# Two transformer blocks in float32 on one core: the input projections as seven block products, with their weight sums and the parameter loads moved

## What is computed

```python
# first block
x = x + 0.5 * swiglu(rms_norm(x, ffn1_norm), ffn1_w_gate, ffn1_w_up, ffn1_w_down)
proj = rms_norm(x, mix_norm) @ w_in          # 1024 x 7880: 4808 attention columns, 3072 gates
x = x + token_mixer(...)                     # three attentions on the columns of proj
x = x + 0.5 * swiglu(rms_norm(x, ffn2_norm), ffn2_w_gate, ffn2_w_up, ffn2_w_down)
# second block
x = layer_norm(x, ln_in_g, ln_in_b)
for l in range(2):
    h = x @ w_in_2[l]                        # 1024 x 1976
    cq, ckv, kr, nq, kc, vc, ks, vs, kw, vw, gl = jnp.split(h, split_at, axis=-1)
    x = layer_norm(ALPHA * x + mix(cq, ckv, ...) @ w_out[l], ...)
    x = layer_norm(ALPHA * x + memory_cross_attn(x, memn, ...), ...)
    x = layer_norm(ALPHA * x + conv_ffn(x, ...), ...)
```

## Time and profile before

| | |
|---|---|
| median of three runs | 1939.09 us (1938.17 to 1942.79) |
| the profiled execution | 1933.61 us |
| its span, first to last instruction | 1931.8 us |
| TensorE busy | 1837.9 us, 95% |
| VectorE, ScalarE, GpSimd busy | 835.2, 320.9, 152.1 us |
| mean granted TensorE clock | 0.972 of full speed |
| moved by DMA | 265.39 MB, 137 GB/s over the span |

### The profile page before, as it was taken

The page is one execution under the profiler, slowest core; times in us unless marked ns, Lnnn a source line. Parts: engine busy times, 40 slices in busy tenths (PEclk is TensorE's granted clock), DMA queues, the critical chain, the costliest instruction groups (busy, mean ns, idle before and its releaser), DMA issues.

```text
span 1931.8 us, 18805 instructions
## 1 busy us (share of the span) xinstructions
PE 1837.9 (95%) x7094; PEld 1240.4 (64%) x7094; DVE 835.2 (43%) x1907; ACT 320.9 (17%) x790; POOL 152.1 (8%) x111
## 2 busy tenths in 40 slices
PE   7999999989899999998999989999989999999997
PEld 6886444534747885446866758884448766578863
DVE  6775400243654776402730125573305520344564
ACT  1111000140601110112611210000123501210000
POOL 1221100000000222300000000001300000000010
PEclk9999999989999999997999999999997999999999
DMA  9554444511155554535034235444533053154540
GB/s 319 183 175 145 166 146 143 179 65 66 45 194 170 160 171 152 199 90 181 2 109 167 95 109 167 138 169 153 164 95 129 1 196 131 44 196 133 173 152 22
DMA packets 162489, 265.39 MB, mean 137 GB/s; under 512 B 4009, under 2 KB 105685, under 8 KB 162271
## 3 DMA queue, kind: packets, MB, share of 16 engines
q1 hardware_dynamic: 157470, 248.18, 38.2%
q0 software_dynamic: 4768, 15.48, 2.4%
q10 hardware_dynamic: 160, 0.52, 0.1%
HBM read 262.56 MB, written 1.08 MB: 136 GB/s over the span
## 4 chain that ended last, share of the span: by engine, by line
PE 90%; ACT 4%; DVE 3%; issue 1%; DVEq 1%; DMA 1%; SPq 1%; ACTq 0%
PE psum L679 22%; PE psum L704 18%; PE psum L742 14%; PE psum L802 13%; PE psum L714 7%; PE psum L920 3%; PE psum L955 3%; PE psum L853 2%; PE psum L691 2%; PE psum L937 2%; PE psum L841 1%; ACT x_t L1191 1%; PE psum L1129 1%; ACT work L1191 1%; DMA ring<-in_ffn_w_up_dram 1%
## 5 line engine op out<-in xcount | busy, mean ns | idle before, releaser
L679 PE MATMUL psum<-x_t,ring 128*128 128x256 f32 x1664 | 364.1, 382 | 4.2 <-ACT x_t L1191 4.2
L679 PEld LDWEIGHTS psum<-x_t,ring 128*128 128x128 f32 x1664 | 318.6, 192 | 49.3 <-ACT x_t L1191 5.4
L704 PE MATMUL psum<-ring,x_t 128*128 128x512 f32 (+2 forms) x672 | 283.9, 585 | 0.0
L704 PEld LDWEIGHTS psum<-ring,x_t 128*128 128x128 f32 x672 | 129.1, 194 | 152.8 <-issue 152.8
L802 PE MATMUL psum<-ring,work 128*128 128x512 f32 x352 | 160.9, 592 | 0.0
L574 POOL TENSOR_TENSOR work<-ring,work 128x1024 f32<-128x1024 f32 (+1 forms) x42 | 102.7, 2445 | 682.7 <-DVE work L1584 682.7
L714 PE MATMUL psum<-ring,x_t 128*128 128x512 f32 x320 | 140.0, 595 | 7.4 <-ACT x_t L1191 7.4
L802 PE MATMUL psum<-work 128*128 128x512 f32 x264 | 122.5, 592 | 0.0
L802 PEld LDWEIGHTS psum<-ring,work 128*128 128x128 f32 x352 | 66.6, 190 | 81.0 <-issue 80.8
L1700 DVE CUSTOM_DVE_ANT_0 work<-psum,work 128x256 f32<-128x256 f32 (+1 forms) x96 | 31.4, 364 | 194.5 <-PE psum L920 194.5
L714 PEld LDWEIGHTS psum<-ring,x_t 128*128 128x128 f32 x320 | 60.0, 190 | 81.5 <-issue 71.8
(11 more groups left out here) (224 smaller groups left out, 1988.1 us busy)
## 6 DMA issues: line engine op xcount, KB each, us to landing
ring<-in_ffn_w_up_dram SPq DMA_DIRECT2D x66, 1024.0 KB, 7.8
ring<-in_w_in_dram SPq DMA_DIRECT2D x21, 2048.0 KB, 7.9
ring<-in_ffn_w_down_dram SPq DMA_DIRECT2D x20, 2048.0 KB, 7.9
ring<-in_ffn_w_gate_dram SPq DMA_DIRECT2D x22, 1024.0 KB, 5.5
ring<-in_xa_wkv_dram SPq DMA_DIRECT2D x8, 2048.0 KB, 9.4
ring<-in_w_out_dram SPq DMA_DIRECT2D x6, 2048.0 KB, 7.8
ring<-in_xa_wq_dram SPq DMA_DIRECT2D x4, 2048.0 KB, 7.7
ring<-in_xa_wo_dram SPq DMA_DIRECT2D x4, 2048.0 KB, 7.9
```

The lines of the kernel that those rows point to most:

```text
L679: last = mm(o[:, c * T:(c + 1) * T], ring[:, n % RING, k * 512 + c * P:k * 512 + (c + 1) * P], acts[:, k, :], start=(k == 0), stop=(k == K ...
L704: last = mm(o[:, i * 512:i * 512 + width], acts[:, k, i * P:(i + 1) * P], ring[:, n % RING, c:c + width], start=(k == 0), stop=(k == kk - 1))
```

## The change

- `project` takes the place of `rows_entry` and `rows_stationary` for nine panels of the first block and three of each layer. It has the heads and tails of `expand`, without hidden rows. `last_columns` makes the 200 and the 440 columns as before, in banks 6 and 7.
- ScalarE copies product 1 of each panel (256 columns) and VectorE writes all the other columns to `P1` or `P2` (`project` under VectorE); `two_at` writes two places with one instruction.
- The first panel's weight sums get buffers of their own (`APART`: `W_MEM`, `W_MEM + 1024`, `W_L`) and are formed before the gathering adds. The second panel's come after the sums of the rows, each other one two panels ahead. A fourth buffer holds the sum that was in place.
- The four batches of turned rows at an entry use banks 4, 5, 4, 3.
- GpSimd makes the new fourth sums, does its clears after the third panel of a layer (in the first block, after the ninth), and issues the twelve parameter loads (now `parameters(l)`) after the first block's attention for layer 0, and after the second gain loads of layer 0 for layer 1.
- A layer's norm of the latent columns on VectorE comes after all three panels. ScalarE takes its root before it copies the last columns. The first heads wait for `group_free` of the third panel only.

```diff
@@ -112,8 +112,9 @@
     if B_H1 <= b < B_N2 or B_H2 <= b < E_X:
         return 4
-    if b in (B_N1 + 3, B_N3 + 3):
-        return 3
+    for b0 in (B_N1, B_N2, B_N3) + tuple(E_X + B_LAYER * l for l in range(LAYERS)):
+        if b0 <= b < b0 + 4:
+            return (4, 5, 4, 3)[b - b0]
     if b >= E_X and (b - E_X) % B_LAYER in (E_X1 - E_X, E_X1 - E_X + 1, E_X2 - E_X, E_X2 - E_X + 1):
         return 6 + (b - E_X) % 2
...
+WINS, LWINS = 9, 3
+F_UP1, F_DN1, F_WIN = 0, UPS, UPS + DOWNS
+F_UP2 = F_WIN + WINS
+F_DN2 = F_UP2 + UPS
+F_LWIN = F_DN2 + DOWNS
+F_DN = F_LWIN + LWINS
+F_LAYER = LWINS + DOWNS
+C_UP1, C_WIN, C_UP2, C_LWIN = 0, UPS, UPS + WINS, 2 * UPS + WINS
+A_UP1, A_WIN, A_UP2, A_LWIN = 0, 2, 4, 6
 FOURTH_ON_VECTOR = (F_UP1, F_UP1 + 1, F_UP2, F_UP2 + 1)
-FORM_PANELS = list(range(P_UP1, P_UP1 + UPS + DOWNS)) + list(range(P_UP2, P_UP2 + UPS + DOWNS)) + \
-    [L_DN + N_LAYER * l + d for l in range(LAYERS) for d in range(DOWNS)]
+APART = (F_WIN, F_LWIN, F_LWIN + F_LAYER)
+FORM_PANELS = list(range(P_UP1, P_WIN + WINS)) + list(range(P_UP2, P_UP2 + UPS + DOWNS)) + \
...
+        def row_corners(j):
+            c = corners(j)
+            return {1: c[1], 2: c[2], 6: c[6], 5: c[7], 7: c[5], 3: c[4], 4: c[3]}
+        def two_at(o1, o2):
+            v = W[:, o1:o1 + 256]
+            return bass.AP(v.tensor, v.offset, [list(v.ap[0]), [o2 - o1, 2], [1, 256]])
...
+            if f in APART:
+                return [w(o, chunks // 2, pitch // 2) for o in (W_MEM, W_MEM + 1024, W_L)]
...
-            pool.wait_ge(panel_done, P_WIN)
+            pool.wait_ge(panel_done, P_WIN + WINS)
...
             pool.dma_start(w(V_ALIBI, 2048), a["c_alibi"]).then_inc(t_in, 16)
+            parameters(0)
...
-            fourth_sums(range(F_UP2, F_DN))
+            fourth_sums(range(F_UP2, F_LWIN))
             for l in range(LAYERS):
-                if l:
-                    pool.wait_ge(panel_done, N_FIRST + N_LAYER * l)
-                else:
-                    pool.wait_ge(turned, B_MEM + 4)
-                    pool.wait_ge(panel_done, N_FIRST)
+                fourth_sums(range(F_LWIN + F_LAYER * l, F_DN + F_LAYER * l))
+                pool.wait_ge(panel_done, L_WIN + N_LAYER * l + LWINS)
                 nc.gpsimd.memset(W[HD:P, V_QTN:V_QTN + 8 * T], 0.0)
...
+                    if k == 1 and l + 1 < LAYERS:
+                        parameters(l + 1)
...
+            def project(n0, count, f0, g0, c0, a0, turn_tile, l=None):
+                n0, g0 = at(n0, N_LAYER, l), at(g0, G_LAYER, l)
+                acts = stationary(XT, XS, 0)
+                def product(j, p):
+                    rhs = moving(f0 + j, n0 + j, KD, 512)[p]
+                    for i in range(KD // 2):
+                        last = mm(row_corners(j)[p], acts[p][:, i, :], rhs[:, i, :], start=(i == 0), stop=(i == KD // 2 - 1))
+                    return last
+                def head(j):
+                    arrived(n0 + j)
+                    group(g0 + j)
+                    pe.wait_ge(first_out, c0 + j)
+                    product(j, 1).then_inc(first_done, 1)
+                    product(j, 2)
+                def tail(j):
+                    pe.wait_ge(forms_ready, f0 + j + 1)
+                    if j == 0:
+                        pe.wait_ge(acts_ready, a0 + 1)
+                    product(j, 6).then_inc(part_done, 1)
+                    if j == 0:
+                        pe.wait_ge(acts_ready, a0 + 2)
+                    product(j, 7)
+                    product(j, 5).then_inc(part_done, 1)
+                    pe.wait_ge(fourth_ready, f0 + j + 1)
+                    product(j, 4)
+                    product(j, 3).then_inc(panel_done, 1)
+                turn_tile(0)
+                head(0)
+                turn_tile(1)
+                head(1)
+                tail(0)
+                tail(1)
+                for j in range(2, count):
+                    head(j)
+                    tail(j)
+                pe.wait_ge(first_out, c0 + count)
+            def last_columns(n, g, width, l=None):
+                n, g = at(n, N_LAYER, l), at(g, G_LAYER, l)
+                arrived(n)
+                pe.wait_ge(group_free, g - 1)
+                for i in range(TT):
+                    for k in range(KD):
+                        last = mm(bank(6 + i)[:, 0:width], XT[:, k, i * P:(i + 1) * P],
+                                  ring[:, n % RING, k * 512:k * 512 + width], start=(k == 0), stop=(k == KD - 1))
...
-            rows_entry(P_WIN, G_WIN, 512, lambda i: turn_tile(B_N2, 3, 3, i))
-            for j in range(1, 9):
-                rows_stationary(P_WIN + j, [G_WIN + j], XT, KD, 512, 512)
-            rows_stationary(P_WIN + 9, [G_WIN + 9], XT, KD, 512, 200)
+            project(P_WIN, WINS, F_WIN, G_WIN, C_WIN, A_WIN, lambda i: turn_tile(B_N2, 3, 3, i))
+            last_columns(P_WIN + 9, G_WIN + 9, 200)
...
-                rows_entry(L_WIN, H_WIN, 512, turn_tile_of(E_X, X, 13, 9, l), l)
-                for j in range(1, 4):
-                    rows_stationary(L_WIN + j, [H_WIN + j], XT, KD, 512, min(512, N_LIN - 512 * j), l)
+                project(L_WIN, LWINS, F_LWIN + F_LAYER * l, H_WIN, C_LWIN + LWINS * l, A_LWIN + 2 * l, turn_tile_of(E_X, X, 13, 9, l), l)
+                last_columns(L_WIN + 3, H_WIN + 3, N_LIN - 1536, l)
                 pe.wait_ge(p_in, at(PARAMS, PARAMS, l))
                 for j in range(2):
                     batch(E_CW + j, [CW[0:88, j, :]], l)
-                pe.wait_ge(group_free, at(H_WIN + 4, G_LAYER, l))
+                pe.wait_ge(group_free, at(H_WIN + 3, G_LAYER, l))
                 for j in range(4):
                     batch(E_NSA + j, [P2[:, i, D_NQ + (2 * j + s) * HD:D_NQ + (2 * j + s + 1) * HD] for s in range(2) for i in range(TT)], l)
                 for j, c in enumerate((D_KC, D_VC, D_KS, D_KW)):
+                    if j == 2:
+                        pe.wait_ge(group_free, at(H_WIN + 4, G_LAYER, l))
                     batch(E_NSA + 4 + j, [P2[:, i, c + s * HD:c + (s + 1) * HD] for s in range(2) for i in range(TT)], l)
                 pe.wait_ge(rows_ready, at(16, PER_Y, l))
...
+            def project_copies(k, b0, count, c0, l_norm=None, l=None):
+                def first(j):
+                    act.wait_ge(first_done, c0 + j + 1)
+                    copy(W[:, TEMPS + 1024 * (j % 2):TEMPS + 1024 * (j % 2) + 256], corners(j)[1]).then_inc(first_out, 1)
+                rstd(k, 1, l_norm)
+                turned_rows(b0, XT, l, range(2))
+                rstd(k + 1, 1, l_norm)
+                first(0)
+                turned_rows(b0, XT, l, range(2, 4))
+                for j in range(1, count):
+                    first(j)
...
-                s1, s2, s4 = sums
+                s1, s2, s4 = sums[0:3]
+                s3 = sums[3] if len(sums) == 4 else even[:, :, a2]
                 v.tensor_tensor(s1, even[:, :, a2], odd[:, :, a2], ALU.add)
                 dr()
                 mid = v.tensor_tensor(s2, s1, even[:, :, a1], ALU.subtract)
                 dr()
-                v.tensor_tensor(even[:, :, a2], even[:, :, a1], even[:, :, a2], ALU.subtract)
+                v.tensor_tensor(s3, even[:, :, a1], even[:, :, a2], ALU.subtract)
                 return mid, v.tensor_tensor(s4, odd[:, :, a1], s2, ALU.subtract)
...
+            def project(f0, count, g0, c0, columns, row, b_last_turn):
                 dve.wait_ge(turned_out, b_last_turn)
                 mid, last = act_sums(XT, XS, 0)
+                mid.then_inc(acts_ready, 1)
+                last.then_inc(acts_ready, 1)
+                weight_sums(f0 + 1, KD, 512)
+                two = lambda x: x.rearrange("p (a b) -> p a b", a=2)
+                for j in range(count):
+                    o, t, c = row_corners(j), TEMPS + 1024 * (j % 2), columns + 512 * j
+                    x, y, z = [two(bank(b)) for b in ((0, 1, 2) if j % 2 == 0 else (6, 7, 3))]
+                    first, u2, u43 = W[:, t:t + 256], W[:, t + 256:t + 512], two(W[:, t + 512:t + 1024])
+                    dve.wait_ge(first_out, c0 + j + 1)
+                    dve.wait_ge(part_done, 2 * (c0 + j) + 1)
+                    v.tensor_tensor(two_at(c, t + 256), first[:, None, :].to_broadcast([P, 2, 256]), x, ALU.add)
+                    dr()
+                    dve.wait_ge(part_done, 2 * (c0 + j) + 2)
+                    v.tensor_tensor(u43, u2[:, None, :].to_broadcast([P, 2, 256]), y, ALU.add)
+                    dr()
+                    v.tensor_tensor(W[:, row + c + 256:row + c + 512], u43[:, 1, :], o[5], ALU.add)
+                    dve.wait_ge(panel_done, FORM_PANELS[f0 + j] + 1)
+                    v.tensor_tensor(two_at(c + 256, row + c), u43, z, ALU.add).then_inc(group_free, 1)
+                    if j + 2 < count:
+                        weight_sums(f0 + j + 2, KD, 512)
+            def network(g0, f0, c0, h0, b_last_turn, h_batch, then=lambda: None):
...
                 down_sums(F_DN1, d)
```

(47 more changed lines are left out.)

93 lines of the change are left out of this document (43 added, 50 removed).

## The result

The changed kernel takes 1916.19 us, median of four runs (1914.66 to 1920.00), against 1940.25 us for the kernel before, run beside it (four runs, 1938.17 to 1942.79): 0.9879 of the time, 95% interval 0.9862 to 0.9895. The forecast was 1916.7. The profiled execution took 1916.15 us for a span of 1914.3.

The account below looks back on a forecast made before the run. TensorE, busy for 95% of the span, was taken as the bound. Gains of 14.9 (first block) + 3.9 + 3.9 (layers) - 0.3 (entries) = 22.4 us, taken from the median 1939.09, gave 1916.7 us; range 1909 to 1926.

Parts of the forecast that it names:

- A panel in the new form, 12.09 us: Projections on TensorE: 28 matmuls of 256 columns take 12.09 us as in `expand`, 1.64 us saved on a full panel.
- scattered write: VectorE's `two_at`: no row of its own, bounded from 0.68 us (L1628) to twice that; taken at the row's, hidden.
- First block: First block's projection: 130.99 us before, 116.11 us in the new form, 14.9 us saved.
- Layers: Each layer's projection: 54.99 us before, 51.11 us in the new form, 3.9 us saved, twice.
- The norm's 1.14 us: Layer entry: 1.14 us of TensorE's wait before the second head, 6.48 us after the first, is for VectorE's norm.
- The first panels' weight sums: Ahead of the gathering adds on VectorE: three sums of 1.23 us, 3.8 us, mostly covered; 0.3 us charged in all.
- If this cover were gone, the whole 3.8 us would stand in front of each entry, 11 us: Projection entries: without TensorE's late product hiding the first weight sums, 3.8 us each would show, 11 us in all.
- Room of 15.5 us: Mid-stream: weight sums are wanted 15.5 us after they start and need 4.5, or 7 with GpSimd's sum; cost nothing.
- Parameters, clears, latent norm at nothing: Moved parameter loads, GpSimd's clears behind the third panel, and the layers' latent-column norm were each charged nothing.
- Rival, clock at the layer entries: Granted clock falls at the layer entries, in thin stretches around the heads; price 6.8 us, 1923.5 us; chance 0.08.
- From execution to median: Whole kernel: the median, 1939.09 us, lies 5.5 us above the profiled execution; 1911.2 from the execution, 1916.7 from the median.
- the sum of 22.4 us: Whole kernel's gain: 14.9 for the first block, 3.9 for each layer, less 0.3 for the entries.

Follow-up runs that it names:

- e1: First block's nine panels in the new form, layers' projections as in the kernel before; 1923.25 us against 1937.15 for the kernel before, 0.993.
- e7: Changed kernel with both heads multiplied before the second tile is turned, tail(0) beginning with product 4; 1913.15 us, 0.9877 of the kernel before.
- e3: Changed kernel with the first panel's weight sums formed after the activation sums, not ahead of the gathering adds; 1926.89 us, 0.9951 of the kernel before.
- e10: Changed kernel with six extra weight sums on VectorE in each first-block panel from the third on; 1926.67 us, 0.9943 of the kernel before.
- e6: Kernel before with only the parameter loads moved one attention sooner; 1938.30 us, 1.0002 of the kernel before.
- the repetition: Changed kernel measured once more with no edit; 1917.52 us against 1936.92 for the kernel before, 0.9902.
- e4: Changed kernel with the first panel's weight sums behind the first gathering add instead of ahead of it; 1921.69 us, 0.9918 of the kernel before.

## Why the prediction was right, point by point

- **A panel in the new form, 12.09 us**: as taken from `expand`, in all fifteen. The "scattered write" takes 0.69 us, the row it was bound to below.
- **First block**: 116.11 forecast, 116.18 measured, gain 14.8 for 14.9. Alone, at equal clock, 15.4 (e1), within the scatter of it.
- **Layers**: 51.11 forecast, 51.22 measured; second head after 6.49 us for 6.48. The norm's 1.14 us was read rightly as a wait of its own: e7 fills it and gets 1.15 back.
- **The first panels' weight sums**: the step that failed. "Three of 1.23 us" was taken from rows in which GpSimd idles; here its last small sum starts between VectorE's, and the charge was 0.3 where the entries lost 0.92. It came to 0.6 us. The row that could have told it stood in the text, for another place. The rule stood there too: in this case the Trainium skill (SBUF — State Buffer, on the two separate sides) has the two engines exclude each other for a whole instruction if VectorE reads two inputs there. The trace agrees: the second sum ends at 216.75 + 2.13 = 218.88, 1.08 behind GpSimd's end at 217.80. It also agrees where the rule names no conflict: the first gathering add, with one input in PSUM, starts at 220.09 beside GpSimd's 2.37 us and makes its way undelayed.
- **"If this cover were gone, the whole 3.8 us would stand in front of each entry, 11 us"**: 9.4 (e3). The sums meet `head(1)`, not the entry.
- **Room of 15.5 us**: wrong for the first chain, which has 12.09 (e10); with 3.8 to 7 in use it made no difference.
- **Parameters, clears, latent norm at nothing**: nothing (e6; L2054 under L848).
- **Rival, clock at the layer entries**: did not come in the changed kernel's two profiles; the chains from the second head on run at the full rate. It is real: one of 14 such entries had it (e3, layer 0), with products 1.7 us longer, half of the 3.4 that the forecast priced.
- **From execution to median**: the 5.5 us between the profiled execution and the median were carried over unexplained. They were right to carry: that execution stood at 0.972, and 0.004 of clock are 6.4 us.

So the sum of 22.4 us is good by its large terms. By place it is 1.0 high (21.4): 0.6 from the locked sums and the rest small differences in the three stretches. At equal clock the runs give 22.7, good to about 1 us, so they can't tell the two apart. That the forecast met the median within 0.5 us is partly luck: the repetition gave 19.4 between medians.

## What to carry to other kernels

Where a kernel already contains the new form, its stream prices the change to a few hundredths of a microsecond; the care belongs to the seams, where it has to be asked for each operation which engine it now runs beside. Sums that stand in the shade of another engine's work cost nothing up to an edge, which is the engine's own time a panel against TensorE's: here nothing was lost at some 10.2 of 12.09 us, and 1.9 us a panel at 13.99. The first panel after a seam has the least room. When the expected gain is near the spread of the runs, hold time against granted clock before explaining a difference, and read an earlier start in one trace as scatter until other traces repeat it.

## What the runs showed of the hardware

- Run to run, the time of this kernel follows the mean granted clock, 1.6 us for each 0.001, from 1930 us at 0.973 to 1942 at 0.966; the same program has this spread.
- Behind a wait of 3.2 us of TensorE at an entry the granted clock fell in two cases of two in which it had not fallen just before (e3, first block and layer 1), and cost 1.7 and 1.4 us beyond the wait. In one of 14 layer entries it fell without such a wait (e3, layer 0: 0.50, the next 16 records 5.41 us for 3.72); the other 13 had 1.00 there, with the same instructions.
- VectorE with two inputs in SBUF and GpSimd made each other wait (VectorE's sum 2.13 us for 1.23, GpSimd's 2.18 for 1.27), at all three contractions with the new sums; set apart in e4, both had their old length again.
